# Chunk-causal attention on eight cores: exponentials as the stationary operand, output by query rows

## The reference

```
k_pos, q_pos: positions; chunk 64
s = einsum('bqhd,bkhd->bhqk', q, k) * 96 ** -0.5
visible = (k_pos // 64) <= (q_pos // 64)
p = softmax(where(visible, s, -inf), axis=-1)
o = einsum('bhqk,bkhd->bqhd', p, v)
```

## Time and profile before

| | us |
|---|---|
| median of 3 runs | 4578.33 |
| lowest, highest | 4577.51, 4910.06 |
| the profiled execution, span of its slowest core | 4587.0 |
| spans of the eight cores | 4535.8 to 4587.0 |
| PE busy | 3826.4 |
| ACT busy | 1849.2 |
| DVE busy | 1804.4 |

### The profile page before, as it was taken

How to read it: one execution, slowest core, us unless ns; L and a number is a source line. 1 busy time by engine, 2 the same in 40 slices (tenths; PEclk the granted TensorE clock), 3 DMA queues, 4 the chain that set the end, 5 groups by cost and what they waited for, 6 DMA issues and landing times.

```text
span 4587.0 us, 62374 instructions; the slowest of 8 cores (4535.8 to 4587.0 us)
## 1 busy us (share of the span) xinstructions
PE 3826.4 (83%) x20039; PEld 1736.3 (38%) x20039; DVE 1804.4 (39%) x2628; ACT 1849.2 (40%) x3057; POOL 479.9 (10%) x573
## 2 busy tenths in 40 slices
PE   3777889898988889368898898997997988979977
PEld 1333433333333333233343443443443443434433
DVE  2554655555555464223333233234133323331330
ACT  2444278787888878121312212212213122122121
POOL 0000000000000000011210200210211112102102
PEclk7888699999999999689999799998998999999989
DMA  5322122423324230764243243342442442334322
GB/s 105 114 92 79 29 42 42 76 42 59 59 48 70 42 58 8 257 241 165 92 168 135 95 153 129 130 174 92 156 165 96 162 156 101 148 129 148 142 106 92
DMA packets 165803, 504.36 MB, mean 110 GB/s; under 512 B 28112, under 2 KB 105136, under 8 KB 121968
## 3 DMA queue, kind: packets, MB, share of 16 engines
q1 hardware_dynamic: 113152, 432.78, 27.2%
q0 software_dynamic: 52336, 67.59, 8.1%
HBM read 503.50 MB, written 87.19 MB: 129 GB/s over the span
## 4 chain that ended last, share of the span: by engine, by line
PE 42%; DVE 8%; ACT 4%; issue 3%; DMA 2%; SPq 0%; POOL 0%; DVEq 0%; ACTq 0%; POOLq 0%
PE psfC L261 41%; ACT junkC L270 3%; DVE tmpf L297 2%; DVE XTm L284 2%; DMA wr<-wsc 1%; ACT statC L268 1%; DVE actT L274 1%; DVE XTm L274 1%; DVE omT L274 1%; PE psbC L264 1%; DVE xnC L278 0%; SPq L258 0%; DVE tmpf L284 0%; ACT L268 0%; POOL mT L274 0%
## 5 line engine op out<-in xcount | busy, mean ns | idle before, releaser
L261 PE MATMUL psfC<-actT,wr 128*128 128x512 bf16 (+3 forms) x6272 | 1213.4, 355 | 54.1 <-DMA wr<-wsc 20.7
L268 ACT ACTIVATE PT<-psS 128x1024 bf16<-128x1024 f32 (+1 forms) x1232 | 1060.8, 940 | 295.4 <-PE psS L261 254.1
L261 PEld LDWEIGHTS psfC<-actT,wr 128*128 128x128 bf16 x6272 | 570.4, 102 | 669.8 <-issue 144.3
L261 PE MATMUL psAcc<-PT,Vb 128*128 128x512 bf16 (+3 forms) x2304 | 663.4, 370 | 105.9 <-DVE PT L294 103.6
L261 PE MATMUL psS<-Qb,Kb 96*128 96x512 bf16 (+1 forms) x2304 | 672.4, 375 | 40.9 <-DVE Vb L291 35.1
L270 ACT ACTIVATE junkC<-XTm 128x1024 bf16<-128x1024 f32 (+1 forms) x132 | 139.5, 1056 | 979.5 <-DVE statC L294 533.0
L268 ACT ACTIVATE tmpf<-psfC 128x512 f32<-128x512 f32 (+1 forms) x432 | 238.7, 555 | 606.4 <-PE psfC L261 556.5
L261 PE MATMUL psfC<-wr,hid 128*128 128x512 bf16 (+1 forms) x2112 | 471.6, 387 | 9.6 <-DMA wr<-wsc 9.6
L297 DVE RECIPROCAL RC<-psAcc 64x512 f32<-64x512 f32 (+1 forms) x144 | 438.9, 3048 | 83.4 <-PE psAcc L261 75.2
L274 POOL TENSOR_TENSOR hid<-tmpf 128x512 bf16<-128x512 f32 (+1 forms) x288 | 273.1, 958 | 973.4 <-ACT tmpf L268 765.7
L261 PEld LDWEIGHTS psAcc<-PT,Vb 128*128 128x128 bf16 x2304 | 200.0, 98 | 424.9 <-issue 285.5
(11 more groups left out here) (143 smaller groups left out, 2992.1 us busy)
## 6 DMA issues: line engine op xcount, KB each, us to landing
wr<-wsc SPq DMA_DIRECT2D x328, 1024.0 KB, 6.0
xt<-x_p SPq DMA_DIRECT2D x8, 2048.0 KB, 11.6
XTm<-x_p SPq DMA_DIRECT2D x8, 2048.0 KB, 11.7
y_p<-XTm POOLq DMA_DIRECT2D x8, 2048.0 KB, 7.1
wsc<-w_in POOLq DMA_DIRECT2D x10, 1024.0 KB, 16.6
qscn<-qn SPq DMA_DIRECT2D x64, 128.0 KB, 1.8
Qb<-qscn SPq DMA_DIRECT2D x16, 512.0 KB, 6.2
osc<-OT SPq DMA_DIRECT2D x128, 64.0 KB, 1.9
```

What stands on the lines that cost most here:

```text
L261: P.emit('pe', lambda e: e.matmul(out, lhsT=lhsT, rhs=rhs, start=start, stop=stop), reads, writes)
L268: P.emit('act', lambda e: e.activation(out=out, in_=in_, func=func, bias=bias, scale=scale), reads, writes)
```

## The change

P times V changes sides. The stationary operand is now a 128x128 block of the exponentials (128 keys by 128 queries), and V streams with a single column of ones, 65 columns. The output stands by query rows: psAcc holds up to four groups of 65 columns, one for each 128 queries, and the sum is the last column of each. The reciprocal covers one element per partition and group, the multiply is 4 x 64 wide with that element broadcast, and its result goes to a buffer OTK that holds the pair of heads side by side. After the odd head of a pair the four 128x128 blocks are transposed on TensorE into psT, copied into OT (128x512), and written by one DMA for both heads. For PSUM the scores keep two buffers psS instead of three; one bank psG takes the K and V pieces and one psT the transposes. Vb and Vs shrink to 66 columns. The weight conversions are paced on the odd head's output.

```diff
--- before.py
+++ after.py
@@ -260,6 +260,10 @@
         def mm(out, lhsT, rhs, start, stop, reads, writes):
             P.emit('pe', lambda e: e.matmul(out, lhsT=lhsT, rhs=rhs, start=start, stop=stop), reads, writes)
 
+        def mms(out, lhsT, rhs, start, stop, reads, writes):
+            P.emit('pe', lambda e: e.matmul(out, lhsT=lhsT, rhs=rhs, start=start, stop=stop, skip_group_check=True),
+                   reads, writes)
+
         def tr(out, in_, ident, reads, writes):
             P.emit('pe', lambda e: e.transpose(out, in_, ident), reads, writes)
 
@@ -601,24 +605,27 @@
             with ExitStack() as sB:
                 def sbb(name, shape, dt):
                     return sB.enter_context(nc.sbuf_tensor(name, list(shape), dt))
-                Vb = [sbb("Vb%d" % i, [128, 32, 128], BF16) for i in range(2)]
-                VsB = [sbb("Vs%d" % i, [128, 9, 128], BF16) for i in range(2)]
+                Vb = [sbb("Vb%d" % i, [128, 32, 66], BF16) for i in range(2)]
+                VsB = [sbb("Vs%d" % i, [128, 9, 66], BF16) for i in range(2)]
                 Qb = [sbb("Qb%d" % i, [96, T], BF16) for i in range(2)]
                 QsB = [sbb("Qs_sb%d" % i, [96, TS], BF16) for i in range(2)]
                 PT = [sbb("PT%d" % i, [128, 1024], BF16) for i in range(4)]
-                RC = [sbb("RC%d" % i, [64, 512], F32) for i in range(2)]
-                OT = [sbb("OT%d" % i, [64, 512], BF16) for i in range(2)]
-                psS = [sB.enter_context(nc.psum_tensor("psS%d" % i, [128, 1024], F32)) for i in range(3)]
+                RC = [sbb("RC%d" % i, [128, 4], F32) for i in range(2)]
+                OT = [sbb("OT%d" % i, [128, 512], BF16) for i in range(2)]
+                OTK = sbb("OTK", [128, 33, 2, 64], BF16)
+                psS = [sB.enter_context(nc.psum_tensor("psS%d" % i, [128, 1024], F32)) for i in range(2)]
+                psG = sB.enter_context(nc.psum_tensor("psG", [128, 512], F32))
+                psT = sB.enter_context(nc.psum_tensor("psT", [128, 1024], BF16))
                 psAcc = [sB.enter_context(nc.psum_tensor("psAcc%d" % i, [128, 512], F32)) for i in range(2)]
-                SP_ = RR([(psS[i], 'psS%d' % i) for i in range(3)])
+                SP_ = RR([(psS[i], 'psS%d' % i) for i in range(2)])
                 AP_ = RR([(psAcc[i], 'psAcc%d' % i) for i in range(2)])
-                GP_ = SP_
+                GP_ = RR([(psG, 'psG')])
                 PTR = RR([(PT[i], 'PT%d' % i) for i in range(4)])
                 ORR = RR([(RC[i], OT[i], 'RCOT%d' % i) for i in range(2)])
-                mset('dve', Vb[0][:, :, 64:128], 1.0, ['Vb0'])
-                mset('dve', Vb[1][:, :, 64:128], 1.0, ['Vb1'])
-                mset('dve', VsB[0][:, :, 64:128], 1.0, ['Vs0'])
-                mset('dve', VsB[1][:, :, 64:128], 1.0, ['Vs1'])
+                mset('dve', Vb[0][:, :, 64:66], 1.0, ['Vb0'])
+                mset('dve', Vb[1][:, :, 64:66], 1.0, ['Vb1'])
+                mset('dve', VsB[0][:, :, 64:66], 1.0, ['Vs0'])
+                mset('dve', VsB[1][:, :, 64:66], 1.0, ['Vs1'])
                 conv_list = list(pan_spec.values()) if conv else []
 
                 def emit_conv(k, paced_on):
@@ -721,17 +728,32 @@
                             done[bi] = 0
                         acc, ac = accs[bi]
                         pt_, pc = pend.pop(i)
+                        npq = min(nq, 128)
                         for hf, (kt, nk, c0, diag) in enumerate(grp):
                             first = done[bi] == 0
                             done[bi] += 1
                             last = done[bi] == n
-                            mm(acc[:, c0:nq], Vbuf[0:nk, kt, :], pt_[0:nk, hf * 512 + c0:hf * 512 + nq], first, last,
-                               [(vcell, kt // 8), vcell, pc], [ac])
+                            for qs in range(c0 // 128, (nq + 127) // 128):
+                                mms(acc[0:npq, qs * 65:qs * 65 + 65],
+                                   pt_[0:nk, hf * 512 + qs * 128:hf * 512 + qs * 128 + npq], Vbuf[0:nk, kt, 0:65],
+                                   first and qs == 0, last and qs == (nq + 127) // 128 - 1,
+                                   [(vcell, kt // 8), vcell, pc], [ac])
                         if done[bi] == n:
                             rc, ot, oc = ORR.get()
-                            recip(rc[0:64, 0:nq], acc[64:128, 0:nq], [ac], [oc])
-                            tt('dve', ot[0:64, 0:nq], acc[0:64, 0:nq], rc[0:64, 0:nq], ALU.mult, [ac, oc], [oc])
-                            dma('sp', odst(q0, nq), ot[0:64, 0:nq], [oc], [('osc', h)])
+                            ns = (nq + 127) // 128
+                            o0 = q0 // 128 if nq == 512 else 32
+                            av = acc[0:npq, 0:ns * 65].rearrange("p (s c) -> p s c", c=65)
+                            recip(rc[0:npq, 0:ns].unsqueeze(2), av[:, :, 64:65], [ac], [oc])
+                            otk = ('otk', o0, h % 2)
+                            tt('dve', OTK[0:npq, o0:o0 + ns, h % 2, :], av[:, :, 0:64],
+                               rc[0:npq, 0:ns].unsqueeze(2).broadcast_to([npq, ns, 64]), ALU.mult, [ac, oc], [otk])
+                            if h % 2 == 1:
+                                for s_ in range(ns):
+                                    tr(psT[:, s_ * 128:s_ * 128 + npq],
+                                       OTK[0:npq, o0 + s_, :, :].rearrange("p a b -> p (a b)"),
+                                       ident[0:npq, 0:npq], [('otk', o0, 0), otk, 'ident'], ['psT'])
+                                cp('dve', ot[:, 0:nq], psT[:, 0:nq], ['psT'], [(oc, 't')])
+                                dma('sp', odst(q0, nq), ot[:, 0:nq], [(oc, 't')], [('osc', h)])
 
                     pieces = list(pieces)
                     every = max(1, (len(items) - 4) // (len(pieces) + 1)) if pieces else 0
@@ -755,10 +777,10 @@
                 krc_s = [('Ks_r', c) for c in range(9)]
 
                 def odst_p(h):
-                    return lambda q0, nq: osc[h // 2][(h % 2) * 64:(h % 2) * 64 + 64, q0:q0 + nq]
+                    return lambda q0, nq: osc[h // 2][:, q0:q0 + nq]
 
                 def odst_s(h):
-                    return lambda q0, nq: osc_s[h // 2][(h % 2) * 64:(h % 2) * 64 + 64, q0:q0 + nq]
+                    return lambda q0, nq: osc_s[h // 2][:, q0:q0 + nq]
 
                 def gen_s(h):
                     i = h % 2
@@ -783,7 +805,7 @@
                                        (qscn, qscr), T)
                     attn_head(h, Kb[i], 'Kb%d_n' % i, krc_p[i], Vb[i], 'Vb%d' % i, Qb[i], 'Qb%d' % i, pblocks,
                               odst_p(h), nxt)
-                    emit_conv(3 * h, [('osc', h)])
+                    emit_conv(3 * h, [('osc', h if h % 2 else h - 1)])
                 if 'B' in phases:
                     P.run(final=('C' not in phases))
                 else:
```

## The result

The changed kernel takes 4631.32 us (median of 4 runs, 4624.43 to 4798.88) against 4577.92 (4577.1 to 4910.06) for the one before on the same chip: a ratio of 1.0108, 95% interval 1.0088 to 1.0128. It is slower by some 50 us. The forecast had it 18 us faster; the time lies in the range, with the other sign. Every kernel here also has executions in which the cores of one half of the chip show a lower granted clock and take some per cent longer; ratios leave these out, and where too few others were measured no ratio is given.

A forecast was written before the change was run, and what follows sets the result against it. TensorE and ScalarE were taken as balanced, neither full, in prompt heads, with ScalarE's floor 61.6 of 79.2 us. Prompt heads -66, sample heads +53, small terms -3 - 2 gave -18: 4569 profiled, 4560 as median; range 4440 to 4700.

The forecast's parts named there:

- rival 2: P times V: small matmuls run at their weight load's rate, 98 ns, making TensorE the bound; 4870 us, chance 0.12.
- rival 1: Prompt heads: ScalarE's 0.90 us rate holds, the psS wait and the pieces cost nothing; 4467 us, chance 0.17.
- rival 3: Prompt heads: TensorE, partly idle, is granted 1.2 GHz, P-times-V matmuls at 0.053 us each; 4910 us, chance 0.03.
- The sample stage's +53: Sample stage and related: pieces in series through psG +34, head 0's pieces +13, first five +2, odd-head transposes +4 us.
- an even head 72.3, an odd one 5.5 more: Prompt heads: average 75.1 us per head against 79.2 before, -66 us over 16 heads.
- Odd heads only: Odd prompt heads: transposes delay the next scores, 4.1 us for seven blocks plus 1.4 at the head's end.
- the memsets' queueing goes with it: Block ends: VectorE's work shrinks from 4.1 to 0.7 us, and the mask memsets no longer queue.
- Sum: an even head: Even prompt head: ScalarE floor 61.6, loop 3.4, block ends 3.2, pieces 2.4, head's end 1.7; 72.3 us.
- the loop: Inner steps of prompt heads: two score buffers make a step 0.96 instead of 0.90 us, 3.4 us per head.
- -66 + 53 - 5 = -18: Whole kernel: prompt heads -66, sample stage +53, small terms -3 and -2; 18 us faster.
- -3 - 2: Small terms: shorter Vb and Vs memsets at the start save 3 us, a shorter last block's end 2 us.
- none was waited for here: Output DMAs: they halve in number and double in partitions, and none was waited for in the kernel before.

The follow-up runs named there:

- Experiment 2: Kernel before with only the score memory split: two score buffers instead of three, K and V pieces in a bank of their own; ratio 1.0201 to before.
- experiment 4: Changed kernel with sample-stage K and V pieces alternating between psG and psT's bank; no ratio, lowest 4604.1 us, sample stage 105 us instead of 142.
- experiment 5: Changed kernel with the weight conversions paced as before, three behind each prompt head; no ratio, lowest 4622.5 us.
- experiment 1: Changed kernel with the four transposes of a block, their copy and DMA issued two steps later; ratio 0.993 to the kernel before, about 4546 us.
- experiment 6: Changed kernel with transposes two steps later and three score buffers shared with pieces and transposes; ratio 0.9788 to the kernel before, 4472.28 to 4496.19 us.
- Experiment 7: Kernel before with only the small diagonal-block memsets moved from VectorE to GpSimd; ratio 1.0209 to the kernel before.
- experiment 3: Changed kernel with three score buffers shared by K and V pieces and transposes, no psG or psT; ratio 0.998 to before, about 4569 us.
- experiment 8: Changed kernel with late transposes, three score buffers, one accumulator, one bank for prompt pieces and transposes, sample pieces in score buffers; ratio 0.9809 to before, lowest 4488.2 us.

## Why the prediction was wrong

**Right, by its own steps.** P-times-V matmuls are 30 ns apart (eight from 1028.59 to 1028.83 above; 29 forecast), so rival 2 falls. The Trainium skill's figure of 81 ns (TensorE: Matmul & The Clock Gate, Back-to-back issue gap) is not what this trace shows: of the slowest core's 880 runs of eight such matmuls the median has 30.4 ns from start to start, and 95% are under 32. The same section's formula for a single matmul's gap, columns over 2.4 plus 2.5 ns, gives 29.6 at 65 columns and agrees. Wide exponentials start 0.92 and 0.99 us apart in turn, 0.955 per step (0.96 forecast), and rival 1's 0.90 falls for two buffers. The clock held 0.95 (rival 3 falls). VectorE's block end is 0.18 and 0.42. The sample stage's +53 was 54 to 60. Experiment 2 shows that the split alone makes some 50 of it, and experiment 4 that pieces in series through psG make 36. The conversions cost the sample stage nothing (experiment 5).

**The step that failed is the sum for a prompt head: "an even head 72.3, an odd one 5.5 more".** An even head took 75.0 (median of the cores) and an odd one 7.9 more. The first error is 2.7 us in all 16 heads, some 40 us; the second 2.4 in eight heads, some 20. The mechanisms were those that the prediction names; their sizes were too small.

**"Odd heads only" (20 us of the miss).** It put 5.5 us on an odd head; experiment 1 takes the transposes out of the way and the odd head loses 8 (83 to 75.2), and even ones lose 1, so their place in the queue costs some 8 us. Inside a head I had 0.59 us lost per block, and the trace shows 1.18 at the block above: counted from its last wide exponential (1024.09, 0.92 before the narrow one), the next scores started at 4.07 and could have at 2.89 (the next wide exponential started at 1.72 and lasts 1.02, plus 0.15). I had 3.67 and 3.08. Of the difference of 0.59, 0.32 is the last P times V (at 2.63 instead of 2.31), held by the memsets behind the K cast: I had counted "the memsets' queueing goes with it", and what goes is only the queueing behind the reciprocal. 0.19 is that scores behind a narrow exponential start earlier than I had them, so that the buffer wait covers less; 0.08 lies in the latencies. In the sum: half of the cover that I took for the transposes was not there. That block is one of the worse: by the exponentials' starts, odd head less even head, the seven blocks of that head lose 1.0 on average, and the head's end 0.8 (gaps of 2.95 and 2.17 above) where I had 1.4. So 8 instead of 5.5.

**"Sum: an even head" (40 us of the miss).** It is small and everywhere. An even head was to take 72.3 and takes 74.4 to 75.7, some 2.5 over. Experiment 1 splits that. Its even head from 924.23 to 997.61 takes 73.4, and by the starts of its exponentials, less ScalarE's rate, it loses 3.1 us in the loop (3.4 forecast), about 0.51 at each of seven block ends, 3.6 (3.2 forecast), 2.25 at the head's end (1.7 forecast), and the rest, about 3, at the pieces (2.4 forecast; 0.54 and 0.46 less the slack of 0.29, as written there, give 2.7). Each term but the loop is a little larger than its rows gave. The change as made adds 1 to 2 us that the late transposes take away too, part of it at the head's start (the gap before its third exponential is 0.77, in experiment 1's head 0.40) and part in single stalls as this one, which TensorE begins with no wait that the trace names:

```profile
967.61 0.60 PE L261 MATMUL psS<-Qb,Kb 96*128 96x512 bf16 x2 [1.13 <-issue]
...
968.36 1.02 ACT L272 ACTIVATE PT<-psS 128x1024 bf16<-128x1024 f32 x1 [1.47 <-PE psAcc L264]
```

Why late transposes in the odd heads spare the even ones such stalls is open. With late transposes, three shared buffers bring the even head from 73.9 to 71.7 (experiments 1 and 6), so two buffers cost it about 2 us.

**The sum in the end.** Forecast -66 + 53 - 5 = -18. Measured: sample stage +54 to +60, prompt stage about -3 by the medians of the cores (some 2.5 over forecast in all 16 heads, 40, and some 2.5 more in the eight odd ones, 20), total about +55, where the runs' medians differ by 53. Both terms had the right sign; what was missed in the larger, negative one turned the whole, and neither of its two errors alone would account for the measured sum. The "-3 - 2" of small terms can't be told from the scatter between cores.

**Where the gain lies.** Experiment 6 keeps the new P times V, removes the transposes' wait and the split, and its prompt heads take 100 us less than those of the kernel before, at a sample stage some 13 longer. That is the worth of the change's main part; as made, it was spent on queue position (some 75 us, 64 of them in the odd heads) and on buffers (some 20 in the prompt heads, 45 in the sample stage).

**Open.** How the 100 us divide between TensorE's saving and VectorE's short reciprocal is not settled. Experiment 7 gives two heads: 2.5 and about 5.5 us came from the memsets alone. If the other heads lay between these, VectorE's part would be some 40 to 90 us (an estimate from those two heads); no run has the short reciprocal without the new P times V. Why the odd heads of experiment 6 still take 3.3 us more than the even ones was not tried; their transposes take a score buffer, and extra gaps of about 1 us stand at the second or third step after a block's end.

## What to carry to other kernels

Before moving work to the end of a block, ask what stands behind it in its engine's queue: an operation that waits for another engine belongs a step or two later, behind work that is ready. A buffer taken from a rotation is paid where the rotation is already tight, which may be a short stage that the change isn't about; price that stage by itself. When several terms of opposite sign nearly cancel, check each cover (which queue, which operation ahead) at one real block of the trace, since half a microsecond per block decides the sign.

## What the runs showed that was not expected

TensorE stops now and then with no wait that the trace names. In the changed kernel it does so for 2 us or more (2.2 to 7.1) on five of the eight cores, seven times in all:

```profile
1307.10 0.38 PE L264 MATMUL psAcc<-Vb,PT 128*128 128x65 bf16 x4 [5.18 <-issue]
1307.29 1.04 PE L261 MATMUL psS<-Qb,Kb 96*128 96x512 bf16 x2
...
1308.13 0.64 PE L264 MATMUL psAcc<-Vb,PT 128*128 128x65 bf16 x8
...
1312.18 0.61 PE L261 MATMUL psS<-Qb,Kb 96*128 96x512 bf16 x2
```

After it the matmuls run at 1.2 GHz for about 5 us (granted clock 0.52 from 1307.0 to 1312.2; scores and eight P times V in 1.29 us, 1307.29 to 1308.58, against 0.67), and TensorE then sets the pace. At that clock eight P-times-V matmuls take 0.46 us, 57 ns each: rival 3's price (53) was nearly right, only its place was not. All seven stops fall in heads 8 and 10. In this kernel six weight conversions run together in each even head, and the DMA share of this core is 0.73 to 0.87 in heads 2 to 12 of even number and 0.06 or less in the odd ones. In experiments 3, 4 and 6, paced alike, every such stop also stands in an even head; experiments 1 and 8, paced alike too, have none of 2 us. That speaks for the DMA traffic as part of the cause; nothing tests it.

The kernel before has no stop of 2 us without a named wait. Its own long heads (up to 84 us) have something else, seen here on core 2:

```profile
658.76 3.36 DVE L297 RECIPROCAL RC<-psAcc 64x512 f32<-64x512 f32 x1 [3.39 <-DMA osc<-OT]
...
663.65 0.59 PE L261 MATMUL psS<-Qb,Kb 96*128 96x512 bf16 x2 [3.80 <-DVE Vb L291]
```

The reciprocal waits 3.39 us until an earlier output has left its buffer, a V cast stands behind it, and the next scores wait 3.80 us for the cast. So "none was waited for here" (the output DMAs, in the prediction) holds for the head that was read and not for all.

The two-buffer loop is not even: exponentials start 0.92 and 0.99 us apart in turn, in the changed kernel and in experiment 2, whether P times V is 8 matmuls or 2.
